# The down matrix by seven block products instead of plain tiles, with its block sums formed in the up stage

## The chip, the cores and the metric

The kernel runs on one core of one Trainium2 chip. The metric is the device time of one execution in microseconds (us). A run of the kernel before took 1713.6 us (median of 3 runs, 1712.56 to 1714.36).

## The reference, cut to what matters

The reference is a decoder block over 1024 tokens of width 1024: two kinds of attention, gates, an output projection, and then a two-matrix network with a squared ReLU. All is float32. What bears on this change is the last part:

```
h = _rms_norm(x, norm_mlp_g)                     # (1024 tokens, 1024)
x = x + square(relu(h @ w_up)) @ w_down          # w_up 1024 x 4096, w_down 4096 x 1024
return _rms_norm(x, norm_final_g)
```

Call U = square(relu(h @ w_up)) the hidden matrix, 4096 rows (transposed: hidden features are rows, tokens are columns) by 1024 tokens.

## The kernel before

Everything is kept transposed, features on the 128 partitions and tokens along the free axis. A float32 product is made from three matrix products of rounded parts: each operand X is split into X_hi (a rounded copy, made by ScalarE) and X_lo = X - X_hi (made by VectorE), and hi·hi + hi·lo + lo·hi is summed in PSUM. So "three matmuls of 128x512" is the unit of work: one 128x128 block of weights against 512 tokens.

**The up stage** (1021 to 1338 us in the trace) works in 16 blocks, n = 0 to 15, each of 256 hidden features. Each block is a 2x2 block product (2 halves of 128 features, 2 halves of the 1024 tokens, the inner 1024 cut in 2 halves of 512) done with Strassen's method in Winograd's form: seven block products P1 to P7 in place of eight. A product is 4 inner tiles x 3 parts = 12 matmuls (`product`, L1084). Their order over the blocks is in `up_products`: in block n it is P1(n), P7(n-1), P3(n-2), P6(n), P4(n-1), P2(n), P5(n). Inputs: the four weight blocks a11, a12, a21, a22 are loaded, VectorE forms four sums of them (`sums`, L1856), ScalarE makes the hi parts of three groups (`form_hi`, L1443) and VectorE the lo parts (`form_lo`, L1886). Outputs: running sums sit in PSUM. ScalarE copies P1 (`copy_s1`, L1451), P1+P6 (`copy_s2`, L1459) and P1+P6+P7 (`copy_s3`, L1467) out. VectorE adds them up, applies ReLU and the norm's factor (`up_c22`, `up_r22`, `up_c12`, `up_r12`, `up_r21`, `up_r11`), ScalarE squares (L1471), and SyncE's queue stores the four 128x512 results of each block to the DRAM buffer `hidden`. Every engine runs its list in the written order, and a wait holds back all that is behind it on its engine.

**The down stage** (1338 to 1686 us) is plain: 8 chunks of 512 hidden features, and in each 8 output tiles of 128 features: 4 inner tiles x 3 parts x 2 token halves = 24 matmuls per tile (L1118), 64 tiles, 1536 matmuls. Hidden tiles come back from DRAM (`load_hidden`), are split (`hidden_hi` L1491, `hidden_lo` L1856), the weights likewise (`weights_hi` L1487, `weights_lo` L1856). VectorE adds each tile into the residual in `keep` (L1856). In the last chunk ScalarE squares the finished tiles (L1570) and VectorE sums the squares into `f_acc`. Then a short tail forms the final norm: `facc` complete, 8 small matmuls, root and reciprocal, 64 transposes (L1130), eight scaled results and their stores.

Of the kernel before, what the change touches and what calls it, by code (L numbers as in the profile page):

```python
# [25 lines left out]
ALU = mybir.AluOpType  # L26
ACT = mybir.ActivationFunctionType
BF16 = mybir.dt.bfloat16
F32 = mybir.dt.float32
# [3 lines left out]
P = 128  # L33
# [30 lines left out]
DN_PAIRS = (3, 2, 1, 0)  # L64
DN_BANKS = (1, 3, 0, 2)
# [3 lines left out]
def up_products(n):  # L69

    if n == 0:
        order = [(0, P1), (0, P2), (0, P6), (0, P5)]
    elif n < UP:
        order = [(n, P1), (n - 1, P7), (n - 2, P3), (n, P6), (n - 1, P4), (n, P2), (n, P5)]
    else:
        order = [(n - 1, P7), (n - 2, P3), (n - 1, P4), (n - 1, P3)]
    return [x for x in order if x[0] >= 0]


PRODUCT = {x: i + 1 for i, x in enumerate(x for n in range(UP + 1) for x in up_products(n))}  # L80
A_FORMS = [(0, 0), (0, 1), (0, 2), (1, 0), (1, 1)]
for _n in range(1, UP):
    A_FORMS += [(q, b) for q, b in ((_n + 1, 0), (_n, 2), (_n + 1, 1)) if q < UP]
A_FORM = {x: i + 1 for i, x in enumerate(A_FORMS)}
H_FORMS = [(w, k) for k in range(3) for w in ("b11", "b21", "t2")]
H_FORMS += [("b11", 3), ("t13", 0), ("t13", 1), ("t13", 2), ("t4b", 0), ("b21", 3), ("t2", 3), ("t13", 3), ("t4b", 1),
            ("t4b", 2), ("t4b", 3)]
H_FORM = {x: i + 1 for i, x in enumerate(H_FORMS)}

# [92 lines left out]
def build(nc, x, g_attn, w_in, b_forget, w_branch, w_out, g_mlp, w_up, w_down, g_final, rope, f_rows, x_mid, hidden, out):  # L182
# [4 lines left out]
    w_dn_v = w_down.rearrange("(f p) n -> p f n", p=P)  # L187
# [3 lines left out]
    with ExitStack() as ctx:  # L191
# [23 lines left out]
        up_t4b = [at(f"up_t4b_{k}", [P, 2, 2, HALF], F32R, 32 + 8 * k) for k in range(4)]  # L215
# [6 lines left out]
        W_KB = (184, 192, 80, 88)  # L222
        dn_w = [at(f"dn_w{i}", [P, 2, 1024], F32R, W_KB[i]) for i in range(4)]
        dn_w_raw = [at(f"dn_w_raw{i}", [P, 1024], F32, W_KB[i] + 4) for i in range(4)]
        HID_KB = (64, 72, 96, 104, 0, 8, 16, 24)
        dn_h = [at(f"dn_h{i}", [P, 2, 1024], F32R, HID_KB[i]) for i in range(8)]
        dn_h_raw = [at(f"dn_h_raw{i}", [P, 1024], F32, HID_KB[i] + 4) for i in range(8)]
        f_sq = [at(f"f_sq{i}", [P, 1024], F32, 168 + 4 * i) for i in range(2)]
        f_acc = at("f_acc", [P, 1024], F32, 176)
        f_g = at("f_g", [P, 1024], F32, 180)  # L230
        y_tile = [at(f"y{i}", [P, 1024], F32, (144, 148, 152, 156, 160, 164, 200, 204)[i])[:] for i in range(8)]
# [93 lines left out]
        def bank_b(q):  # L325
            return ps_bank(6 + q % 2)
# [21 lines left out]
        rstd_l, rstd_r = kp[:, 0, left], kp[:, 0, right]  # L348
        s2 = [kp[:, 1, left], kp[:, 1, right]]
        s1 = [kp[:, 2, right], kp[:, 4, right]]  # L350
        s3, u12 = kp[:, 3, left], kp[:, 3, right]
        u11 = [kp[:, 2, left], kp[:, 2, right]]
        u22 = [kp[:, 4, left], kp[:, 4, right]]
        u21 = [kp[:, 5, left], kp[:, 5, right]]
# [87 lines left out]
        x_back = [sem(f"x_back{i}") for i in range(4)]  # L442
# [32 lines left out]
        u21_out = [sem(f"u21_out{i}") for i in range(2)]  # L475
        u12_out = sem("u12_out")
        dw_in = [sem(f"dw_in{i}") for i in range(4)]
        dw_hi = sem("dw_hi")
        dw_lo = sem("dw_lo")
        dh_hi = sem("dh_hi")  # L480
        dh_lo = sem("dh_lo")
        dn_done = sem("dn_done")
        dn_add = sem("dn_add")
# [14 lines left out]
        def _(sp):  # L498
# [50 lines left out]
            def load_a(q, what):  # L549
                e, m = {"a11": (0, 0), "a12": (1, 0), "a21": (0, 1), "a22": (1, 1)}[what]  # L550
                sp.dma_start(a_block(q, what).rearrange("p (k c) -> p k c", k=4),
                             w_up_v[:, 4 * e:4 * e + 4, (2 * q + m) * P:(2 * q + m + 1) * P]).then_inc(a_in[q % 4], 16)

            def load_hidden(f):

                q = f // 2
                if f % 2 == 0:
                    sp.wait_ge(u11_out[q % 2], 16 * (q // 2 + 1))
                    sp.wait_ge(u12_out, 16 * (q + 1))
                else:  # L560
                    sp.wait_ge(u21_out[q % 2], 16 * (q // 2 + 1))
                    sp.wait_ge(u22_out[q % 2], 16 * (q // 2 + 1))
                sp.dma_start(dn_h_raw[f % 8][:], hidden[f]).then_inc(tile_in[f % 8], 16)

            def load_dn(g):
                b, pair = g // 4, DN_PAIRS[g % 4]
                sp.dma_start(dn_w_raw[g % 4][:].rearrange("p (k c) -> p k c", k=4),
                             w_dn_v[:, 4 * b:4 * b + 4, pair * 256:(pair + 1) * 256]).then_inc(dw_in[g % 4], 16)

            def store_u22(q):  # L570
                sp.wait_ge(u22_ok, q + 1)
                sp.dma_start(hidden[2 * q + 1, :, right], u22[q % 2]).then_inc(u22_out[q % 2], 16)

            def store_u12(q):
                sp.wait_ge(u12_ok, q + 1)
                sp.dma_start(hidden[2 * q, :, right], u12).then_inc(u12_out, 16)

            def store_u21(q):
                sp.wait_ge(u21_ok, q + 1)
                sp.dma_start(hidden[2 * q + 1, :, left], u21[q % 2]).then_inc(u21_out[q % 2], 16)  # L580

            def store_u11(q):
                sp.wait_ge(u11_ok, q + 1)
                sp.dma_start(hidden[2 * q, :, left], u11[q % 2]).then_inc(u11_out[q % 2], 16)

            def reload(m):
                for i in range(2):
                    sp.wait_ge(x_out[i], (64, 48)[i])
                sp.dma_start(kp[:, m, :], x_mid[m]).then_inc(x_back[m // 2], 16)
# [10 lines left out]
            for n in range(KC):  # L600
# [12 lines left out]
                else:  # L613
                    if n >= 2:
                        sp.wait_ge(x_out[n % 2], 16 * (n // 2))
                    sp.wait_ge(resid, n + 1)
                    sp.dma_start(x_mid[OUT_ORDER[n]], kp[:, OUT_ORDER[n], :]).then_inc(x_out[n % 2], 16)

            for n in range(UP):
                q = n + 2  # L620
                if q < UP:
                    sp.wait_ge(done, PRODUCT[n, P1])
                    load_a(q, "a11")
                elif n == UP - 1:
# [1526 lines left out]
```

## Time and profile before

| what | value |
|---|---|
| median of 3 runs | 1713.6 us |
| the profiled execution's own time | 1710.07 us |
| its span, first to last instruction | 1708.3 us |
| TensorE (PE) busy | 1623.1 us, 95% |
| VectorE (DVE) busy | 970.9 us, 57% |
| ScalarE (ACT) busy | 749.7 us, 44% |
| mean granted TensorE clock | 0.987 |

The profile lists, for each engine, how long its instructions ran and, where it sat idle, which engine's instruction ended the wait. A matmul of 512 columns shows 389 ns of its own but the next one starts before it ends, so its price is the distance between starts.

### The profile page before, as it was taken

The page shows a single profiled execution, that of the slowest core. Times are in us where ns is not written, and L with a number is a line of the kernel's source. Part 1 is how long each engine was busy: PE and PEld are TensorE (multiplying, and loading weights), DVE is VectorE, ACT ScalarE, POOL GpSimd, SP SyncE. Part 2 cuts the span into 40 slices and gives each one's busy share as a digit, 9 for nine tenths or more (in the row PEclk, how much of TensorE's full clock was granted, in tenths as well). Part 3 has the DMA queues.
Part 4 walks back from the last instruction along what each step waited for, and adds up shares of the span by engine and source line. Part 5 has one row for each costly group of instructions (what it writes and reads, how often), then busy time and mean ns, then how long its engine had stood idle before and what let it go on. Part 6 is the DMA issues. An engine that isn't in the chain of part 4 may idle for free.

```text
span 1708.3 us, 22294 instructions
## 1 busy us (share of the span) xinstructions
PE 1623.1 (95%) x8024; PEld 1337.6 (78%) x8024; DVE 970.9 (57%) x1917; ACT 749.7 (44%) x1602; POOL 4.1 (0%) x20
## 2 busy tenths in 40 slices
PE   6998998997899999999999998999999999999997
PEld 5777776775688887788888887888888888888886
DVE  5688888875666666522215566555555544444445
ACT  6566777783667666511113454433344311111111
POOL 0000000000000000000000000000000000000000
PEclk9999999999899999999999999999999999999998
DMA  5210110010010200011121542333334622222212
GB/s 173 87 38 26 32 32 25 26 38 13 13 51 13 63 26 23 14 54 44 51 60 52 148 124 80 118 119 116 105 105 143 227 99 99 99 99 98 93 33 99
DMA packets 142487, 126.19 MB, mean 74 GB/s; under 512 B 5160, under 2 KB 124968, under 8 KB 142256
## 3 DMA queue, kind: packets, MB, share of 16 engines
q1 hardware_dynamic: 142384, 124.84, 23.0%
q8 instruction: 62, 1.02, 0.2%
q14 instruction: 41, 0.34, 0.1%
HBM read 100.15 MB, written 24.67 MB: 73 GB/s over the span
## 4 chain that ended last, share of the span: by engine, by line
PE 79%; DVE 10%; ACT 5%; issue 5%; DMA 0%; ACTq 0%; DVEq 0%; SPq 0%
PE ps L1118 20%; PE ps L1084 18%; PE ps L759 17%; PE ps L803 12%; PE ps L875 4%; PE ps L842 2%; DVE work L1669 2%; PE ps L853 2%; ACT work L1266 1%; DVE ps L1690 1%; DVE o_nat L1712 1%; ACT tmp L1258 1%; DVE tmp L1654 1%; PE ps L748 1%; DVE work L1697 1%
## 5 line engine op out<-in xcount | busy, mean ns | idle before, releaser
L803 PE MATMUL ps<-hspl,wsp 128*128 128x512 f32 x1536 | 423.1, 408 | 8.4 <-ACT tmp L1222 6.8
L1118 PE MATMUL ps<-dn_h,dn_w 128*128 128x512 f32 x1536 | 348.3, 389 | 0.0
L1118 PEld LDWEIGHTS ps<-dn_h,dn_w 128*128 128x128 f32 x1536 | 288.4, 188 | 59.8
L803 PEld LDWEIGHTS ps<-hspl,wsp 128*128 128x128 f32 x1536 | 266.2, 190 | 54.7 <-ACT tmp L1222 8.6
L759 PE MATMUL ps<-hspl,wsp 128*128 128x512 f32 x960 | 222.6, 392 | 0.6 <-ACT keep L1288 0.6
L759 PEld LDWEIGHTS ps<-hspl,wsp 128*128 128x128 f32 x960 | 181.1, 189 | 38.4 <-issue 0.8
L1856 DVE TENSOR_TENSOR keep<-keep,ps 128x1024 f32<-128x1024 f32 x72 | 87.8, 1220 | 161.0 <-PE ps L1118 146.9
L875 PEld LDWEIGHTS ps<-work 128*128 128x128 f32 x856 | 112.0, 191 | 47.7 <-issue 37.7
L1258 ACT ACTIVATE tmp<-ps,negmax 128x128 f32<-128x128 f32 (+7 forms) x160 | 87.5, 547 | 125.8 <-DVE negmax L1690 123.9
L1697 DVE TENSOR_TENSOR work<-ps,work 128x128 fp32r<-128x128 f32 (+3 forms) x192 | 84.4, 454 | 102.5 <-ACT work L1266 99.9
L875 PE MATMUL ps<-work 128*128 128x128 f32 x856 | 122.5, 276 | 21.2 <-DVE o_nat L1712 20.1
L1084 PE MATMUL ps<-up_b,a_hi 128*128 128x512 f32 x384 | 120.5, 395 | 4.9 <-DVE up_b L1856 3.8
L1241 ACT ACTIVATE work<-tmp 64x128 fp32r<-64x128 f32 x320 | 113.3, 354 | 5.9
L1669 DVE SCALAR_TENSOR_TENSOR work<-tmp,work 64x128 fp32r<-64x128 f32 x320 | 101.3, 317 | 9.2 <-ACT work L1241 1.8
L1491 ACT CAST dn_h<-dn_h_raw 128x1024 fp32r<-128x1024 f32 x32 | 33.3, 1048 | 146.6 <-DMA dn_h_raw<-hidden 146.5
L842 PE MATMUL ps<-work 128*128 128x256 f32 (+3 forms) x384 | 88.8, 326 | 3.1 <-issue 2.1
L1084 PEld LDWEIGHTS ps<-up_b,a_hi 128*128 128x128 f32 x384 | 73.3, 191 | 21.0 <-DVE up_b L1856 4.2
L1471 ACT ACTIVATE keep<-keep 128x512 f32<-128x512 f32 x64 | 40.4, 631 | 98.4 <-DVE keep L2013 41.1
L853 PE MATMUL ps<-ident,tmp 128*128 128x128 f32 x428 | 73.7, 274 | 10.2 <-issue 6.9
L1847 DVE TENSOR_TENSOR wsp<-raw,wsp 128x1024 fp32r<-128x1024 f32 x18 | 22.0, 1223 | 105.9 <-ACT wsp L1386 105.9
L1084 PE MATMUL ps<-up_t,a_hi 128*128 128x512 f32 x256 | 79.1, 390 | 0.0
L1084 PE MATMUL ps<-up_t4b,a_hi 128*128 128x512 f32 x256 | 78.8, 389 | 0.0
(201 smaller groups left out, 2138.7 us busy)
## 6 DMA issues: line engine op xcount, KB each, us to landing
raw<-in_w_in SPq DMA_DIRECT2D x47, 512.0 KB, 3.8
hidden<-keep SPq DMA_DIRECT2D x64, 256.0 KB, 2.3
dn_w_raw<-in_w_down SPq DMA_DIRECT2D x32, 512.0 KB, 3.5
dn_h_raw<-hidden SPq DMA_DIRECT2D x32, 512.0 KB, 6.4
a_raw<-in_w_up SPq DMA_DIRECT2D x36, 256.0 KB, 2.8
spare<-in_w_up SPq DMA_DIRECT2D x28, 256.0 KB, 3.2
keep<-in_x SPq DMA_DIRECT2D x8, 512.0 KB, 7.0
fbias<-f_rows SPq DMA_DIRECT2D x8, 512.0 KB, 4.9
```

Of the source, the lines that this page charges most:

```text
L759: ins = pe.matmul(ps[:, cols], w(wp, k), mv(mp, k)[:, cols], start=(k == 0 and n == 0), stop=(k == ks - 1 and n == 2))
L803: ins = pe.matmul(psp(u, g), wsp[c % 2][:, wp, k * P:(k + 1) * P], hspl[:, mp, k, cols], start=(n == 0), stop=(n == 23), skip_group_check= ...
L842: ins = pe.matmul(oo, lt, rh, start=(m == 0), stop=(m == len(ops) - 1), skip_group_check=True)
L853: ins = pe.transpose(PS[2][:, (u % 2) * HALF + (k - a) * P:(u % 2) * HALF + (k - a + 1) * P], probs(G)[:, k * P:(k + 1) * P], ident[:])
L875: ins = pe.matmul(o, pt[:, G % 2, part, n * P:(n + 1) * P], v_nat[:, j, s % 2, :, :].rearrange("p s d -> p (s d)"), start=(part == 0 and n ...
L1084: ins = pe.matmul(o, a_part(q, j, wp)[:, k * P:(k + 1) * P], b_block(j, mp, k), start=((j in (P1, P5) or j == P2 and q < 2) and k == 0 and ...
L1118: ins = pe.matmul(o[:, cols], dn_w[g % 4][:, wp, a:a + P], dn_h[(4 * b + f) % 8][:, mp, cols], start=(f == 0 and n == 0), stop=(f == 3 and ...
L1241: act.activation(tile_view(q_st[dst:dst + 64, G % 3, 0, :], t), tile_tokens(q_raw(t)[row:row + 64], t, s // 2), ACT.Copy, scale=-QSCALE).t ...
L1258: act.activation(probs(G)[:, 0:n * P], psc[G % 2][:, 0:n * P], ACT.Exp, bias=negmax[:, c:c + 1], scale=-1.0, accum_out=rowsum[:, c:c + 1]) ...
L1669: dve.scalar_tensor_tensor(out=tile_view(q_st[dst:dst + 64, G % 3, 1, :], t), in0=tile_tokens(q_raw(t)[row:row + 64], t, s // 2), scalar=- ...
L1697: dve.tensor_tensor(pt[:, G % 2, 1, a * P:b * P], PS[2][:, (u % 2) * HALF:(u % 2) * HALF + (b - a) * P], pt[:, G % 2, 0, a * P:b * P].bitc ...
L1856: return dve.tensor_tensor(out, a, b, op)
```

## The change

The down matrix gets the same treatment as the up matrix. There are 32 more blocks, n = 16 to 47: 8 chunks of 512 hidden features, and in each chunk 4 blocks of 2x128 output features. One product of a down block has 2 inner tiles x 3 parts = 6 matmuls. One function `product` now serves both stages, and `block_products` gives the order. P5 of all chunks stays in PSUM, where it is summed over the chunks (banks 2 to 5); the four other results (P1+P2 as "11", "22", "12", "21") are added by VectorE to the residual in every block.

The moving inputs of the down products are 7 forms of each chunk of the hidden matrix: four blocks of it (for P1, P2, P3 and, through them, the rest) and four block sums, T1 to T4. The sums are formed in the up stage by VectorE (`t_sums`, four new 128x512 operations in each block) and stored, so `hidden` now has seven 128x512 tiles per block where it had four. `u21` has one buffer instead of two, and the places of the temporaries in `keep` are dealt anew. In the down stage each of the 7 forms of a chunk is loaded (`load_form`, 512 KB), rounded by ScalarE (`dn_hi`, 128x1024) and its remainder formed by VectorE (`dn_lo`, 128x1024). The down weights go through the up stage's `sums`, `form_hi` and `form_lo`, one unit of 1 MB for two blocks. The split of the up matrix's form "t4b", first tile, moves behind `form_lo(1, 1)` on both engines.

```diff
-def up_products(n):
+def block_products(n):
     if n == 0:
+        return [(0, P1), (0, P2), (0, P6), (0, P5)]
+    if n <= UP:
         order = [(n, P1), (n - 1, P7), (n - 2, P3), (n, P6), (n - 1, P4), (n, P2), (n, P5)]
+        order += [(n - 1, P3)] if n == UP else []
+    elif n == UP + 1:
+        order = [(n, P1), (n - 1, P7), (n, P6), (n - 1, P4), (n, P2), (n, P5), (n - 1, P3)]
     else:
+        order = [(n, P1), (n - 1, P7), (n - 1, P3), (n, P6), (n - 1, P4), (n, P2), (n, P5)]
...
+    early = {UP - 1: [(0, P1)], UP: [(0, P6), (0, P2), (0, P5), (0, P7)], UP + 1: [(0, P4), (0, P3), (1, P1)],
+             UP + 2: [(1, P6)], UP + 3: [(1, P2), (1, P5), (1, P7)], UP + 4: [(1, P4), (1, P3)]}
...
+    c, pos = divmod(n - UP, 4)
+    c += 1 if pos else 0
+    if c < 2 or c > 7:
+        return []
+    return [(c, j) for j in ((P3,), (P1, P6, P2), (P5,), (P7, P4))[pos]]
...
         @block.tensor
...
+            def product(n, j):
...
+                down = n >= UP
+                pe.wait_ge(a_lo, A_FORM[form_of(n), form_place(j)[0]])
+                if down and (n - UP) % 4 == 0:
+                    pe.wait_ge(b_lo, D_FORM[(n - UP) // 4, j])
                 if j == P1:
...
+                        pe.wait_ge(c21_ok, n - 1)
...
+                elif j == P4:
+                    if down:
+                        pe.wait_ge(c22_ok, n + 1)
...
+                ks = 2 if down else 4
...
-            for i in range(8 * FF_BLOCKS):
...
         @block.scalar
...
+            copy_s1(UP)
+            dn_hi(0, P6)
             copy_s3(UP - 1)
             square_22(UP - 1)
             square_12(UP - 2)
+            dn_hi(0, P2)
+            copy_s2(UP)
+            dn_hi(0, P5)
+            form_hi(UP, 2)
             square_21(UP - 1)
+            dn_hi(0, P7)
+            copy_s1(UP + 1)
             square_12(UP - 1)
+            dn_hi(0, P4)
...
+            for n in range(UP + 2, NB):
+                forms = dn_forms(n)
+                copy_s1(n)
+                if n % 2:
+                    for x in forms[:2]:
+                        dn_hi(*x)
+                    if form_of(n) + 1 < N_FORM:
+                        form_hi(form_of(n) + 1, 0)
+                        form_hi(form_of(n) + 1, 1)
+                    for x in forms[2:]:
+                        dn_hi(*x)
+                    copy_s2(n)
+                    if form_of(n) + 1 < N_FORM:
+                        form_hi(form_of(n) + 1, 2)
+                else:
+                    for x in forms:
+                        dn_hi(*x)
+                    copy_s2(n)
+                for i in final_events(n):
+                    final_square(i)
...
         @block.vector
...
+            def t_sums(q, ops=(1, 2, 3, 4)):
...
+                        dve.wait_ge(u12_ok, q + 1)
...
+                        ins = add(t3, u22[q % 2], u12, ALU.subtract)
...
+                        ins = add(t2, t3, u11[q % 2])
...
+                        ins = add(u12, u12, u11[q % 2], ALU.subtract)
...
+                        ins = add(t4, u21, t2, ALU.subtract)
...
                 if n >= 2:
                     up_r12(n - 2)
+                    t_sums(n - 2)
                 up_r21(n - 1)
+                form_lo(n + 1, 1)
+                if n == UP - 1:
+                    dn_lo(0, P1)
                 up_r11(n)
+            sums(UP + 1)
+            dn_lo(0, P6)
             up_c22(UP - 1)
             up_r22(UP - 1)
             up_c12(UP - 2)
             up_r12(UP - 2)
+            dn_lo(0, P2)
+            dn_lo(0, P5)
+            t_sums(UP - 2)
             up_r21(UP - 1)
+            dn_add(UP, "11")
+            form_lo(UP, 2)
+            dn_lo(0, P7)
             up_c12(UP - 1)
             up_r12(UP - 1)
+            dn_lo(0, P4)
+            dn_add(UP, "22")
...
+            for n in range(UP + 2, NB + 1):
+                forms = dn_forms(n)
...
+                elif n % 2 == 0:
+                    form_lo(u - 1, 2)
+                    if more:
+                        sums(u, (1,))
+                    if n > UP + 2:
+                        dn_add(n - 1, "22")
+                    if more:
+                        sums(u, (2,))
+                    dn_add(n - 1, "12")
+                    if more:
+                        sums(u, (3, 4))
+                    dn_add(n - 1, "21")
+                    for x in forms:
+                        dn_lo(*x)
+                    dn_add(n, "11")
+                else:
+                    for x in forms[:2]:
+                        dn_lo(*x)
+                    dn_add(n - 1, "22")
+                    if more:
+                        form_lo(u, 0)
+                    dn_add(n - 1, "12")
+                    if more:
+                        form_lo(u, 1)
+                    dn_add(n - 1, "21")
+                    for x in forms[2:]:
+                        dn_lo(*x)
+                    dn_add(n, "11")
+                if NB > n > NB - 4:
+                    dn_last(n - 1, "22")
+                    dn_last(n - 1, "12")
+                for i in final_events(n):
+                    final_sum(i)
...
         @block.sync
...
+            def load_unit(u):
+                sp.wait_ge(a_lo, A_FORM[u - 2, 2])
+                load_a(u, "a21")
+                load_a(u, "a22")
+                sp.wait_ge(done, last_use(u - 2, P1))
+                load_a(u, "a11")
+                sp.wait_ge(done, last_use(u - 2, P2))
+                load_a(u, "a12")
...
+            for n in range(UP + 3, NB):
+                c, pos = divmod(n - UP, 4)
+                if pos % 2 and form_of(n) + 2 < N_FORM:
+                    load_unit(form_of(n) + 2)
+                if pos == 0 and c < 7:
+                    for j in D_ORDER:
+                        load_form(c + 1, j)
```

## Rows read from the trace of the kernel before

**Rows 1.** The page, busy time of each engine over the span, and instructions.
```profile
PE 1623.1 (95%) x8024; PEld 1337.6 (78%) x8024; DVE 970.9 (57%) x1917; ACT 749.7 (44%) x1602; POOL 4.1 (0%) x20
```
**Rows 2.** Busy time by stretch: up stage, down stage, tail (columns: length, engines, clock, DMA, GB/s).
```profile
1021.48:1337.90 316.42, 311.54 (x1377) 257.69 (x1376) 183.70 (x224) 129.81 (x174) 0.00 (x0) 0.99 0.35 115
1337.90:1686.20 348.30, 348.30 (x1537) 288.20 (x1535) 153.30 (x131) 64.91 (x65) 0.00 (x0) 1.00 0.27 96
1686.20:1708.30 22.10, 12.51 (x81) 12.05 (x80) 12.72 (x12) 1.26 (x2) 0.00 (x0) 0.77 0.47 191
```
**Rows 3.** Waits after 1330 us: who waited for whom (total us, times, longest).
```profile
DVE keep L1856 <- PE ps L1118: 146.9, 55, 4.2
```
**Rows 4.** TensorE's two waits in the up stage.
```profile
1030.20 1.22 PE L1084 MATMUL ps<-up_b,a_hi 128*128 128x512 f32 x2 [3.80 <-DVE up_b L1856]
...
1049.46 0.70 PE L1084 MATMUL ps<-up_b,a_hi 128*128 128x512 f32 x2 [1.08 <-ACT keep L1451]
```
**Rows 5.** Instructions of line 1118, the down matmuls.
```profile
L1118 PE MATMUL ps<-dn_h,dn_w x1536: 388/389/389, 1337.9 to 1685.8; 128*128 128x512 f32 x192
```
**Rows 6.** TensorE in order of time: first matmuls of P1(9) and of P7(8).
```profile
1193.74 0.62 PE L1084 MATMUL ps<-up_b,a_hi 128*128 128x512 f32 x2
...
1196.46 0.62 PE L1084 MATMUL ps<-up_t,a_hi 128*128 128x512 f32 x2
```
**Rows 7.** VectorE in order of time in that block (start, length, what, idle before).
```profile
1194.02 0.69 DVE L1856 TENSOR_TENSOR a_raw<-spare 128x512 f32<-128x512 f32 x1 [2.10 <-DMA a_raw<-in_w_up]
1194.74 0.69 DVE L1856 TENSOR_TENSOR spare<-a_raw,spare 128x512 f32<-128x512 f32 x1
1195.35 0.68 DVE L1856 TENSOR_TENSOR a_raw<-a_raw,a_raw 128x512 f32<-128x512 f32 x1
...
1200.67 1.22 DVE L1886 TENSOR_TENSOR a_lo<-a_raw,a_hi 128x1024 fp32r<-128x1024 f32 x1
1201.80 0.69 DVE L2013 SCALAR_TENSOR_TENSOR keep<-keep 128x512 f32<-128x512 f32 x1
...
1204.56 1.76 DVE L1886 TENSOR_TENSOR a_lo<-spare,a_hi 128x1536 fp32r<-128x1536 f32 x1 [1.47 <-ACT a_hi L1443]
...
1207.55 0.69 DVE L2020 SCALAR_TENSOR_TENSOR keep<-ps,keep 128x512 f32<-128x512 f32 x1 [0.63 <-PE ps L1084]
```
**Rows 8.** ScalarE in order of time in that block.
```profile
1196.66 0.57 ACT L1451 COPY ps<-ps 128x512 f32<-128x512 f32 x1 [4.08 <-PE ps L1084]
1197.15 1.05 ACT L1443 CAST a_hi<-a_raw 128x1024 fp32r<-128x1024 f32 x1
...
1203.06 1.47 ACT L1443 CAST a_hi<-spare 128x1536 fp32r<-128x1536 f32 x1
...
1206.95 0.63 ACT L1471 ACTIVATE keep<-keep 128x512 f32<-128x512 f32 x1 [1.54 <-DVE keep L2031]
```
**Rows 9.** The page, DMA issues: kilobytes each, median us from issue to landing.
```profile
hidden<-keep SPq DMA_DIRECT2D x64, 256.0 KB, 2.3
...
dn_h_raw<-hidden SPq DMA_DIRECT2D x32, 512.0 KB, 6.4
a_raw<-in_w_up SPq DMA_DIRECT2D x36, 256.0 KB, 2.8
```
**Rows 10.** VectorE at the head of the up stage.
```profile
1021.24 1.22 DVE L1856 TENSOR_TENSOR up_t4b<-keep,up_t4b 128x1024 fp32r<-128x1024 f32 x1
```
**Rows 11.** Busy time and clock by stretch: an attention stretch, after the long wait, around the short.
```profile
200.00:300.00 100.00, 88.44 (x474) 69.34 (x473) 83.44 (x255) 72.53 (x212) 0.00 (x0) 1.00 0.10 27
...
1030.00:1032.00 2.00, 1.80 (x4) 1.49 (x5) 1.79 (x4) 1.22 (x2) 0.00 (x0) 0.50 0.00 0
...
1048.00:1050.00 2.00, 0.92 (x4) 0.48 (x3) 1.97 (x4) 1.78 (x3) 0.00 (x0) 1.00 0.16 54
```
**Rows 12.** TensorE in order of time at the end: the first small matmul of the mean.
```profile
1689.89 2.31 PE L1124 MATMUL ps<-mean_w,f_acc 128*128 128x1 f32 x16 [3.66 <-DVE f_acc L1856]
```
**Rows 13.** The chain that ended last, in order of time: matmuls after the 3.80 us wait.
```profile
1030.20 6.37 PE ps L1084 x15
```

More of the change, by code:

```diff
@@ L346, in a_block, with dn_tiles, dn_out @@
             return third_raw(q)[:, {"a21": 0, "s3": 0, "a22": 1, "s4": 2}[what], :]
[L348 to L354, printed above, removed]
+        s1 = [kp[:, 0, left], kp[:, 0, right]]
+        u11 = [kp[:, 1, left], kp[:, 4, right]]
+        u22 = [kp[:, 1, right], kp[:, 6, left]]
+        s2 = [kp[:, 2, left], kp[:, 4, left]]
+        s3 = kp[:, 2, right]
+        rstd_l, rstd_r = kp[:, 3, left], kp[:, 3, right]
+        u12, t2 = kp[:, 5, left], kp[:, 5, right]
+        t3 = kp[:, 6, right]
+        u21, t4 = kp[:, 7, left], kp[:, 7, right]
+        def dn_tiles(n):
+            pos = (n - UP) % 4
+            first = pos // 2 * 4 + pos % 2
+            return first, first + 2
+        def dn_out(n, what):
+            return kp[:, dn_tiles(n)[int(what[0]) - 1], (left, right)[int(what[1]) - 1]]
         def to_natural(g, copy, eng):
@@ L474, in build @@
         u22_out = [sem(f"u22_out{i}") for i in range(2)]
[L475 to L483, printed above, removed]
+        u21_out = sem("u21_out")
+        t_ok = sem("t_ok")
+        t1_out = sem("t1_out")
+        t2_out = sem("t2_out")
+        t3_out = sem("t3_out")
+        t4_out = sem("t4_out")
+        b_hi = sem("b_hi")
+        b_lo = sem("b_lo")
+        fin12 = sem("fin12")
+        fin22 = sem("fin22")
         fsq = sem("fsq")
@@ L1081, in product @@
+                first = j == P1 or j == P5 and n < UP + 4 or j == P2 and n < 2
+                o = bank_b(n) if j == P2 else bank_c(n) if j == P5 else bank_e(n) if j == P3 else bank_a(n)
+                ks = 2 if down else 4
+                for k in range(ks):
+                    if n == 0:
                         pe.wait_ge(hf_lo, H_FORM[{P1: "b11", P2: "b21", P6: "t2", P5: "t13", P7: "t13", P4: "t4b",
@@ L1525, in _ @@
             form_hi(1, 1)
-            for k in range(1, 4):
+            for k in range(4):
                 h_hi("t4b", k)
             act.wait_ge(rstd_done, 1)
-            act.copy(kp[:, 0, :], PS[2][:]).then_inc(rstd_out, 1)
+            act.copy(kp[:, 3, :], PS[2][:]).then_inc(rstd_out, 1)
             square_11(0)
@@ L1982, in _ @@
             dve.reciprocal(xrstd[:], xstat[:]).then_inc(rstd_ok, 1)
-            for k in range(1, 4):
+            for k in range(4):
                 h_lo("t4b", k)
@@ new lines, in dn_last, with final_sum @@
+            def dn_last(n, what):
+                dve.wait_ge(done, PRODUCT[n, P5])
+                if what == "12":
+                    dve.wait_ge(c12_ok, n + 1)
+                else:
+                    dve.wait_ge(c22_ok, n + 1)
+                o = dn_out(n, what)
+                add(o, o, bank_c(n)).then_inc(fin12 if what == "12" else fin22, 1)
+            def final_sum(i):
+                half = int(FINAL[i][1][1]) - 1
+                cols = (left, right)[half]
+                dve.wait_ge(fsq, i + 1)
+                if i == 0:
+                    dve.wait_ge(gfin_in, 16)
+                    link(dve.memset(f_acc[:], 0.0))
+                else:
+                    dve.wait_ge(facc, i)
+                add(f_acc[:, cols], f_acc[:, cols], f_sq[:, i % 4, :]).then_inc(facc, 1)
```

547 lines of the change are left out of this document (273 added, 274 removed).

## The prediction

> **What bounds the kernel now.** I read the busy times first: TensorE (PE) works 95% of the span, VectorE 57%, ScalarE 44% [rows 1]. The question is whether that holds in the two stages touched, so next comes the table by stretch: PE is busy 311.5 of 316.4 us in the up stage and for all of the 348.3 us of the down stage, at full clock [rows 2]. Then the waits: in the down stage VectorE waits for PE 55 times, at most 4.2 us [rows 3], and nothing makes PE wait before the end. So down there only fewer or cheaper matmuls count, and PE has cover: VectorE is at 153 of 348 us, ScalarE at 65. The two waits of PE in the up stage are at its head [rows 4].
>
> **Removed.** 64 tiles x 24 = 1536 matmuls took 348.3 us, 0.2268 us each [rows 2, 5]. The new stage has 32 blocks x 7 products x 6 = 1344. The 192 fewer are worth 192 x 0.2268 = 43.5 us. The up stage shows that this price holds when products alternate: P1(9) to P7(8) is 2.72 us for 12 matmuls [rows 6]. A product in the down stage is half of that, 1.36 us, a block 9.53 us.
>
> **What must fit into 9.53 us.** VectorE, for two down blocks (19.05 us): 8 additions, 4 weight sums at 0.69 us, three weight remainders (1.22, 1.22, 1.76), and 3.5 hidden remainders at 1.22 [rows 7]: 5.5 + 2.8 + 4.2 + 4.3 = 16.8 us, 88%. ScalarE: four copies at 0.57, roundings 1.05 + 1.05 + 1.47, and 3.5 at 1.05 [rows 8]: 9.5 us, 50%. Both fit on average; the order decides. Two handovers come from rows: PE's product is seen by ScalarE 0.20 us after the next one starts (1196.46 to 1196.66) [rows 6, 8], by VectorE the same, and a VectorE operation of 512 columns lets the next start after 0.61 us, one of 1024 after 1.13 [rows 7]; on ScalarE a copy of 0.57 gives way after 0.49 [rows 8], and I take 0.95 for a rounding of 1.05.
>
> **An even block** (time 0 is the start of its P1; its slots are P1 to 1.36, P7 of the block before to 2.72, P3 to 4.08, P6 to 5.44, P4 to 6.80, P2 to 8.17, P5 to 9.53). VectorE: third weight remainder, first weight sum, then "22", for which P7 is done at 2.91. The sum waits for the weight block a12, asked for when P2 is done, at -1.2; with 2.8 us to landing [rows 9] it runs at 1.7 to 2.4, "22" at 2.9 to 3.6, and P4, which needs it, starts at 5.44. Slack 1.8 us. "21" ends at 7.7, needed by the next P1 at 9.53. No cost.
>
> **An odd block.** ScalarE first copies P1 (1.55 to 2.12), then rounds two hidden forms (2.04 to 3.09, 2.99 to 4.04). VectorE makes their remainders (3.11 to 4.33, 4.25 to 5.47), and only then "22" (5.39 to 6.08). P4 waits for it: it starts at 6.15 instead of 5.44, 0.7 us late. This is the queue at work: "22" could run at 2.9 but stands behind two remainders, which stand behind ScalarE. After it the weight remainders end at 8.9 and "21" at 9.6, while the next P1 is now due at 10.25. Blocks with two or more early forms: 19, 21, ... 43, that is 13. Cost 13 x 0.72 = 9.4 us. Bounds: 0, if the handovers are shorter than I take them, and 13 x 1.5 = 20 us with every link 0.2 us slower.
>
> **The seam**, blocks 15 to 19, where little can be done ahead because the old stage holds the buffers. I write out the lists of the diff with the durations above; time 0 is the start of P1(16), and old products still last 2.72 us.
> - P1(16) needs the first hidden remainder. "21" of 14 ends 1.8 us before block 15 does, its square takes 0.6, the rounding 1.05, the remainder 1.2: 1.1 us late, with the form's load landing just in time 1.3.
> - P2(16), due at 10.9: VectorE has the sums of unit 17 until 5.1 (a12 lands late, at 2.4), a remainder, "22" of 15, then "12" of 14 until 9.1; its square ends at 9.8, the rounding of form P2 at 10.7, the remainder at 11.95: 1.1 late.
> - P7(16), due at 18.9: four `t_sums` 13.3 to 16.0, "21" of 15, one addition to 17.2, the 1.76 us form to 18.9, the remainder to 20.05: 1.2 late.
> - P4(16), due at 22.8: "12" of 15 to 21.3, its square to 21.95, rounding to 22.9, remainder to 24.1, "22" to 24.75: 2.0 late.
> - P7(17) and P6(18), each behind a ScalarE copy: 0.25 each.
> - P1(19), due at 40.1: "22" of 17 to 34.1, two `t_sums`, a remainder, a form to 38.1, four weight sums and "12" to 41.4, "21" to 42.05: 2.0 late.
>
> Sum 8.1; I take 8.0. Bounds: 0 (no wait of VectorE or ScalarE reaches PE), and 16: a link late by 1 us passes through each of some eight waits, and the reloads of the residual share the DMA with the first forms.
>
> **The up stage.** Added per block on VectorE: four sums of 0.69, 2.8 us, on 10.7 of 19.05 (183.7 of 316.4 us in the stage [rows 2]). They stand ahead of "21", which goes from 1207.55 to about 1211 on the scale of rows 7: the first of them waits for the square of "12", ending at 1207.58 [rows 8], and four follow at 0.61 to 0.72. P1(10) is due at 1193.74 + 19.05 = 1212.8, so 1.1 to 1.8 us of slack are left: no cost. The queue moves too: the load of a12 stands behind the four stores and goes about 1.8 us later, the sums then run at 1195.8, and what follows them waits until 1200 for a ScalarE copy anyway. The stores grow by three of 256 KB per block; each lands in 2.3 us [rows 9], and a buffer is wanted again 19 us later (`u21`, now single: stored at about +18.2, wanted at +35.5). If this cover were gone, it would be up to 15 x 1 us; the lower bound is 0.
>
> **The head.** The first "t4b" remainder leaves its place ahead of the residual addition: 1.14 us [rows 10] less on the path to the 3.80 us wait [rows 4]. The clock was 0.50 after that wait [rows 11]; whether 2.7 us of idleness leave it up, no row says. I take -1.1, bounds -2.5 and 0. The 1.08 us wait stays: its chain starts at PE's spreading of the factor.
>
> **The end.** The last three products P7, P3, P4 of block 47 have a chain: "22", its last part, "12", its last part, "21", then three half-size sums of squares. VectorE comes out of block 47's squares 3.5 us late and holds P4(47) by 1.5 us; from P4's end to the mean it is 3.4 us, before 3.66 [rows 12]; block 46 adds 0.3. Together +1.6, bounds 0 and 4.
>
> **Sum** on the profiled execution: 1708.3 - 43.5 + 9.4 + 8.0 - 1.1 + 1.6 = 1682.7 us of span. Around the span lie 1710.07 - 1708.3 = 1.8, and the median of the runs shown is 3.5 above that execution's own time: 1688.0.
>
> **A rule that speaks against the change.** In an attention stretch PE is busy 88% of 100 us and the granted clock is 1.00; it was 1.00 around the 1.08 us wait, and 0.50 after the 3.80 us one [rows 4, 11]. The Trainium skill, "TensorE: Matmul & The Clock Gate", section "A second HAM failure mode: psum-queue depth-cycling", says that frequent tiny idle gaps between groups of matmuls, with PSUM banks cycled, can make the clock swing between its two levels and cost throughput. By that rule the new down stage, with a gap in every second block, would swing, and the time would be that of rival 4; the attention stretch, idle 12% of the time, speaks against it.
>
> **Rivals.**
> 1. *No new waits*: ScalarE and VectorE keep ahead, the orders cost nothing. 1708.3 - 43.5 - 1.1 + 5.3 = 1669. For it: 12% and 50% of free time. Against it: the chain copy, two roundings, two remainders is longer than 5.44 us by sums of rows. 12%.
> 2. *Weights late*: a12 lands like the hidden loads, 6.4 us after its issue [rows 9], as the forms of the next chunk are asked for right behind it. The first sum then ends at 5.9, "22" at 6.6, P4 is 1.2 us late in each of some 13 even blocks too: +16, 1704. Against it: 2.8 us where other transfers run beside it. 18%.
> 3. *VectorE is the bound*: 16.8 us of work in 19 with gaps forced by waits for PE; if each pair of blocks takes 20.8 instead of 19.8, 16 more: 1704. 8%.
> 4. *The clock falls* (the side of slower): place, the waits of 0.7 to 2 us in the down stage and seam; price, after the long wait 15 matmuls took 6.4 us instead of 15 x 0.227 = 3.4 [rows 13], so 3 us a time. The gain left is 25.6 us: from nine falls in the 20 waits on, the kernel is slower; with all, 1688 + 60 = 1748. Against it: the clock of 1.00 beside waits [rows 11]. 5%.
>
> **Numbers.** Forecast 1688 us (57%; its own range 1679 to 1697), rivals as given. The range, 8 in 10, takes in the bounds on both sides: 1673 to 1705. A measurement tells 0.2%, 3.4 us, from no change: faster 0.93, within 0.02, slower 0.05.
>
> **What would show it.** Right: 1344 matmuls of the down stage at 0.227 us; PE waits of about 0.7 us ahead of P4 in every odd block up to 43, ended by VectorE's addition; seven waits in the seam, 8 us in all; no wait of PE in blocks 2 to 14; the head's wait at 2.7 us. Wrong: waits of ScalarE or VectorE for a12 that reach PE in even blocks (rival 2), waits ahead of P1 (rival 3), clock under 1.0 in the down stage (rival 4), or PE at work without a gap (rival 1).

## The result, and the profile after

The changed kernel takes 1704.34 us (median of 4, 1703.57 to 1705.92) against 1713.98 (median of 4, 1712.56 to 1715.10) before: a ratio of 0.9949, 95% interval 0.9937 to 0.9962. It is faster, as forecast, but by 9.6 us instead of 25.6. The profiled execution has an own time of 1703.57 us and a span of 1701.7.

Busy times on the page of the changed kernel, and its DMA issues (KB each, median us from issue to landing):
```profile
PE 1593.1 (94%) x7832; PEld 1304.0 (77%) x7832; DVE 1114.0 (65%) x2165; ACT 831.9 (49%) x1714; POOL 4.1 (0%) x20
...
dn_raw<-hidden SPq DMA_DIRECT2D x56, 512.0 KB, 5.6
```
192 matmuls are gone [rows 1], as the arithmetic says. The table by stretch (start and end, length, PE, PEld, DVE, ACT, POOL, clock, DMA share, GB/s) puts the three stretches of [rows 2] beside it. The second here begins at P1(16), the first product of the down matrix; four products of the up stage still lie behind it.
```profile
1026.36:1332.38 306.02, 299.78 (x1330) 247.65 (x1328) 212.85 (x276) 124.97 (x164) 0.00 (x0) 0.99 0.44 147
1332.38:1679.33 346.95, 323.79 (x1392) 260.80 (x1392) 267.03 (x326) 151.77 (x185) 0.00 (x0) 0.99 0.43 147
1679.33:1701.70 22.37, 12.95 (x82) 12.01 (x80) 13.35 (x15) 1.44 (x3) 0.00 (x0) 0.82 0.47 188
```
What the reader is to see: before, PE had no idle time in its down stage [rows 2]. Now 23.2 of 347 us of the second stretch are idle, and VectorE's share of it is 77%, where it was 44%.

**A correction before any comparison.** The first product of the up stage starts at 1026.36 us; before, it was 1021.48. PE's work ahead of that point is the same, so these 4.9 us are not of the change. They are clock: in the same stage, which is not touched, the granted clock of six microseconds is 1.00 in the one execution and 0.54 in the other, and PE issues 44 matmuls in it or 25. Over 380 to 472 us PE starts 412 matmuls in the one and 382 in the other, and behind that, 500 to 1020 us, no fewer (2666 and 2676). First the kernel before, then the changed one:
```profile
466.00:472.00 6.00, 6.00 (x44) 5.36 (x42) 3.49 (x10) 3.88 (x12) 0.00 (x0) 1.00 0.01 3
```
```profile
466.00:472.00 6.00, 6.00 (x25) 5.01 (x24) 2.48 (x8) 1.95 (x6) 0.00 (x0) 0.54 0.00 0
```
Over all profiles of this study that point lies between 1021.5 and 1027.7 us. So I count from it on: 1708.3 - 1021.48 = 686.8 us before, 1701.7 - 1026.36 = 675.3 us after. In this pair of profiles the change gives **11.5 us**, the forecast said 25.6, and 14.1 us are to be found. A second profile of the changed kernel (e0 below) has 678.8 us from that point on, 3.5 more, so differences of this size between two profiles show nothing by themselves.

PE's waits in order of time (start, length of the group, engine and line, in brackets the idle time before it and its releaser). The first line is the head's wait, the next eight are the seam:
```profile
1034.17 0.76 PE L1170 MATMUL ps<-up_b,a_hi 128*128 128x512 f32 x2 [2.89 <-DVE up_b L1944]
...
1332.38 0.70 PE L1170 MATMUL ps<-dn_b,a_hi 128*128 128x512 f32 x2 [2.27 <-issue]
...
1345.00 0.71 PE L1170 MATMUL ps<-dn_b,a_hi 128*128 128x512 f32 x2 [1.16 <-issue]
...
1347.92 0.70 PE L1170 MATMUL ps<-dn_b,a_hi 128*128 128x512 f32 x2 [1.30 <-issue]
...
1354.77 0.70 PE L1170 MATMUL ps<-dn_b,a_hi 128*128 128x512 f32 x2 [1.17 <-issue]
...
1359.60 0.70 PE L1170 MATMUL ps<-dn_b,a_hi 128*128 128x512 f32 x2 [1.83 <-DVE keep L1944]
...
1377.20 0.70 PE L1170 MATMUL ps<-dn_b,a_hi 128*128 128x512 f32 x2 [1.83 <-DVE keep L1944]
...
1379.76 0.70 PE L1170 MATMUL ps<-dn_b,a_hi 128*128 128x512 f32 x2 [0.95 <-ACT ps L1526]
...
1388.83 1.19 PE L1170 MATMUL ps<-dn_b,a_hi 128*128 128x512 f32 x2 [4.71 <-DVE keep L1944]
...
1410.79 0.70 PE L1170 MATMUL ps<-dn_b,a_hi 128*128 128x512 f32 x2 [0.63 <-DVE keep L1944]
...
1430.74 0.70 PE L1170 MATMUL ps<-dn_b,a_hi 128*128 128x512 f32 x2 [0.63 <-DVE keep L1944]
```
Behind the head's, they stand ahead of P1(16), P2(16), P5(16), P7(16), P4(16), P1(19), P7(18), P4(18), then P4(20) and P4(22). And PE's waits between 1395 and 1640 us, summed (total us, times, longest):
```profile
PE ps L1170 <- DVE keep L1944: 7.5, 12, 0.6
```
Twelve waits of 0.63 us, one in every second block, ended by VectorE's addition. That is the picture forecast for the odd blocks. The 4.71 us wait was not in the forecast; it is the first of the thirteen odd blocks, 19, and it is also followed by a slower clock: 1.19 us for the first two matmuls instead of 0.70.

### The profile page after: what moved, and what is told of

The parts are those of the page before. It is cut to its first block, busy times and chain, and to the rows that moved or that the text cites. A ratio compares the mean times of both kernels' runs of the same rounds, so it can differ in the third digit from the quotient of the medians.

```text
span 1701.7 us, 22848 instructions
## 1 busy us (share of the span) xinstructions
PE 1593.1 (94%) x7832; PEld 1304.0 (77%) x7832; DVE 1114.0 (65%) x2165; ACT 831.9 (49%) x1714; POOL 4.1 (0%) x20
## 4 chain that ended last, share of the span: by engine, by line
PE 71%; DVE 14%; issue 6%; ACT 6%; DMA 2%; SPq 0%; ACTq 0%; DVEq 0%
PE ps L1170 30%; PE ps L833 17%; PE ps L877 12%; PE ps L949 4%; PE ps L916 2%; DVE work L1757 2%; PE ps L927 2%; DVE keep L1944 1%; DVE dn_b L1944 1%; ACT work L1326 1%; DVE ps L1778 1%; DVE o_nat L1800 1%; ACT dn_b L1554 1%; ACT tmp L1318 1%; DVE tmp L1742 1%
## 5 line engine op out<-in xcount | busy, mean ns | idle before, releaser
L1170 PE MATMUL ps<-dn_b,a_hi 128*128 128x512 f32 x896 | 279.7, 393 | 25.4 <-DVE keep L1944 18.4
L1170 PEld LDWEIGHTS ps<-dn_b,a_hi 128*128 128x128 f32 x896 | 167.3, 189 | 68.9 <-issue 34.0
L1170 PE MATMUL ps<-dn_b,a_lo 128*128 128x512 f32 x448 | 175.2, 391 | 0.0
L1944 DVE TENSOR_TENSOR keep<-keep,ps 128x512 f32<-128x512 f32 (+1 forms) x144 | 101.3, 712 | 35.6 <-PE ps L1170 20.9
L1944 DVE TENSOR_TENSOR dn_b<-dn_raw,dn_b 128x1024 fp32r<-128x1024 f32 x56 | 67.3, 1221 | 50.8 <-ACT dn_b L1554 50.7
L1170 PEld LDWEIGHTS ps<-dn_b,a_lo 128*128 128x128 f32 x448 | 84.5, 189 | 17.9
L1980 DVE TENSOR_TENSOR a_lo<-a_raw,a_hi 128x1024 fp32r<-128x1024 f32 (+1 forms) x66 | 81.3, 1234 | 11.0 <-ACT a_hi L1504 10.9
```

What stands on the lines that cost most here:

```text
L1170: ins = pe.matmul(o, a_part(n, j, wp, k), b_block(n, j, mp, k), start=(first and k == 0 and m == 0), stop=(k == ks - 1 and m == 2), skip_g ...
L1944: return dve.tensor_tensor(out, a, b, op)
L1980: dve.tensor_tensor(a_lo_t[q % 2][b][:], src[:], a_hi_t[q % 2][b][:].bitcast(F32), ALU.subtract).then_inc(a_lo, 1)
```

## The experiments

Each was timed in 5 rounds with the kernel before on the same chip. My theory after the result: the gain went into waits of PE that come from the *order* of VectorE's, ScalarE's and SyncE's lists, not from the amount of work. Its rivals: VectorE has too much to do (its busy time rose by 143 us), or the clock. "From P1(0)" is the profiled span less the start of P1(0), one profile for each; the changed kernel's first profile had 675.3.

| run | median us | ratio to before, 95% | from P1(0) us |
|---|---|---|---|
| before | 1713.0 to 1713.5 | 1 | 686.8 |
| e0_changed_again | 1703.91 | 0.9939 [0.9925, 0.9954] | 678.8 |
| e1_22_first | 1690.78 | 0.9871 [0.9857, 0.9886] | 665.1 |
| e2_forms_early | 1696.16 | 0.9897 [0.9883, 0.9911] | 668.4 |
| e3_hi_first | 1698.57 | 0.9913 [0.9900, 0.9926] | 669.5 |
| e4_three | 1681.86 | 0.9807 [0.9791, 0.9823] | 655.5 |
| e5_p1_form_early | 1702.62 | 0.9944 [0.9931, 0.9957] | 676.1 |
| e6_tsums_1col | 1701.18 | 0.9932 [0.9918, 0.9946] | 672.0 |
| e7_all_five | 1681.57 | 0.9813 [0.9794, 0.9831] | 652.6 |
| e8_p6_form_early | 1677.70 | 0.9795 [0.9780, 0.9810] | 651.1 |
| e9_end_22_first | 1679.36 | 0.9804 [0.9790, 0.9818] | 651.6 |

**e0_changed_again**: the changed kernel once more, for the spread.

> The changed kernel itself, as the yardstick on this chip: about 1704 us, ratio to the kernel before about 0.995. From block 0 to the end of the up stage and on, PE's waits as in its first trace: 12 of 0.63 us in odd down blocks, 4.7 us ahead of P4(18).

Its six runs lie between 1696.80 and 1705.84. The wait ahead of P4(18) was 6.27 us in its profile where it had been 4.71: the size of that wait is not fixed, its place is. From P1(0) on this profile takes 678.8 us, the first one 675.3.

**e1_22_first**: in the odd blocks, the addition that P4 waits for goes ahead of the two remainders.

```diff
+                    dn_add(n - 1, "22")
                     for x in forms[:2]:
                         dn_lo(*x)
-                    dn_add(n - 1, "22")
```

> One thing undone: in odd down blocks VectorE's addition of "22" no longer stands behind two hidden remainders. My theory (the wait is the queue behind ScalarE's two roundings): the 12 waits of 0.63 us, 0.79 from start to start, go, the wait ahead of P4(18) shrinks to nearly nothing too, since "22" of 18 no longer stands behind late forms, but P2/P5-type products of block 20 may then wait for the late forms instead. Steady part alone: 12 x 0.79 = 9.5 us less than the changed kernel, 1695; with the wait ahead of P4(18) and its slow clock up to 16 less, 1688. Rival (VectorE is full, the wait only moves to P1 of the next block): 1702 to 1704.

The ratio falls by 0.0068, some 12 us. The stretch 1400 to 1640 us of the changed kernel, then of this one:
```profile
1400.00:1640.00 240.00, 232.47 (x1013) 188.87 (x1012) 188.16 (x226) 107.16 (x127) 0.00 (x0) 1.00 0.41 141
```
```profile
1400.00:1640.00 240.00, 240.00 (x1058) 197.22 (x1057) 195.07 (x235) 112.33 (x133) 0.00 (x0) 1.00 0.41 136
```
PE has no gap left, with VectorE busy 195 of 240 us (81%) instead of 188. So VectorE's load is not what cost time there: order is, and the rival "VectorE is the bound" falls for this stretch. In block 19 the same edit takes the 4.71 us wait away, but 2.08 us now stand ahead of P7(18) and 2.33 ahead of P1(20): there the late thing is something else (e2).

**e2_forms_early**: five of the second chunk's hidden loads in SyncE's list go ahead of the weight loads of unit 18, and all seven ahead of the last stores and four reloads.

```diff
-            load_form(1, P1)
+            for j in (P1, P6, P2, P5, P7):
+                load_form(1, j)
             load_unit(UP + 2)
+            load_form(1, P4)
+            load_form(1, P3)
...
-            load_form(1, P6)
...
-            for j in (P2, P5, P7, P4, P3):
-                load_form(1, j)
```

> One thing moved: SyncE's queue asks for the seven forms of chunk 1 ahead of the four reloads and the last up stores, some 20 us earlier. My theory (the forms of chunk 1 are late only because they stand behind reloads in the queue): the wait of 4.71 us ahead of P4(18) falls to the 0.6 us of other odd blocks, the clock stays up after it (2.1 us), the 0.95 us ahead of P7(18) goes: 7 us less than the changed kernel, 1697. Rival (the DMA engines are full around the seam, order is nothing): the loads then delay the weights of unit 18 or the reloads, and the time stays within 1 us, 1704.

SyncE's list in the changed kernel (start, length, what): the load asked for first there and the group of five, behind the last stores and reloads.
```profile
1371.69 0.95 SPq L639 DMA_DIRECT2D hidden<-keep  x1
1372.76 0.82 SPq L624 DMA_DIRECT2D dn_raw<-hidden  x1
1374.44 2.46 SPq L652 DMA_DIRECT2D keep<-x_mid  x3
1377.02 3.12 SPq L624 DMA_DIRECT2D dn_raw<-hidden  x5
```
ScalarE there, waiting for these loads to land, and VectorE, waiting for ScalarE:
```profile
1378.08 1.05 ACT L1554 CAST dn_b<-dn_raw 128x1024 fp32r<-128x1024 f32 x1 [8.54 <-DMA dn_raw<-hidden]
...
1384.45 1.04 ACT L1554 CAST dn_b<-dn_raw 128x1024 fp32r<-128x1024 f32 x1 [2.81 <-DMA dn_raw<-hidden]
```
```profile
1385.53 2.55 DVE L1944 TENSOR_TENSOR dn_b<-dn_raw,dn_b 128x1024 fp32r<-128x1024 f32 x2 [4.54 <-ACT dn_b L1554]
1388.00 0.68 DVE L1944 TENSOR_TENSOR keep<-keep,ps 128x512 f32<-128x512 f32 x1
```
The addition at 1388.00 is "22" of block 18, and P4(18) starts at 1388.83. Read backwards: P4(18), "22", two remainders, their roundings, a load that took 8.25 us to land, one of a pile of five. Ahead of that load SyncE's list had to wait for a store to land before it could go on to the last reload. Both in the chain of waits (start, length, what):
```profile
1371.69 4.83 DMA hidden<-keep
...
1377.51 8.25 DMA dn_raw<-hidden
```
In e2 that load is issued some 20 us earlier, in a group of five that starts at 1357.18 us. P4(18) there waits 0.64 us, at full clock, and the wait ahead of P7(18) is gone:
```profile
1384.23 0.70 PE L1170 MATMUL ps<-dn_b,a_hi 128*128 128x512 f32 x2 [0.64 <-DVE keep L1944]
```
The ratio falls by 0.0042, 7 us. What e1 cures at the end of this chain (the addition no longer behind the remainders), e2 cures at its start.

**e3_hi_first**: in the seam, the loads and roundings of chunk 0's forms go one place ahead of stores, copies and squares.

```diff
+            load_form(0, P5)
+            load_form(0, P7)
             store_u22(UP - 1)
-            load_form(0, P5)
-            load_form(0, P7)
...
+            dn_hi(0, P2)
             square_22(UP - 1)
             square_12(UP - 2)
-            dn_hi(0, P2)
-            copy_s2(UP)
             dn_hi(0, P5)
+            copy_s2(UP)
             form_hi(UP, 2)
-            square_21(UP - 1)
             dn_hi(0, P7)
+            square_21(UP - 1)
             copy_s1(UP + 1)
-            square_12(UP - 1)
             dn_hi(0, P4)
+            square_12(UP - 1)
```
(and `load_form(0, P4)` ahead of `store_t(UP - 2)`.)

> Orders at the seam: ScalarE rounds the forms P2, P7 and P4 of chunk 0 ahead of the squares they stood behind, and the loads of P5, P7 and P4 of chunk 0 stand ahead of the stores. My theory (VectorE idles three times 1.6 us there behind ScalarE): the waits ahead of P2(16), P5(16), P7(16), P4(16), 1.3 + 1.5 + 1.3 + 2.0 us, shrink by 3.5 to 5 us in all: 1700. Rival (VectorE's amount of work at the seam is what counts, idling or not): under 1 us, 1703 to 1704.

The waits ahead of P2(16) and P5(16) are gone, those of P7(16) and P4(16) are down from 1.17 and 1.83 to 0.49 and 0.37:
```profile
1332.85 1.19 PE L1170 MATMUL ps<-dn_b,a_hi 128*128 128x512 f32 x2 [2.26 <-issue]
...
1352.77 0.70 PE L1170 MATMUL ps<-dn_b,a_hi 128*128 128x512 f32 x2 [0.49 <-issue]
...
1356.12 0.71 PE L1170 MATMUL ps<-dn_b,a_hi 128*128 128x512 f32 x2 [0.37 <-DVE keep L1944]
```
The ratio falls by 0.0026 only, 4.5 us: the clock fell after the first wait here (1.19 us for two matmuls; from P1(16) to P7(16) PE needs about 1.5 us more than its matmuls and the 0.49 us wait account for), and 2.30 us stand ahead of P7(18), where it had been 0.95.

**e4_three**: the three edits together.

> The three orders of the first experiments together ("22" first in odd blocks, forms of chunk 1 early, roundings at the seam ahead of the squares). If the three costs are separate: the changed kernel's 1704 less 10.3 (13 waits of 0.79), less 7 (late forms and the slow clock after them), less 5: 1681 to 1682. If they share a cause (VectorE at the seam is simply full), less is left than the sum: 1686 to 1690.

The ratio is 0.0132 below that of e0; the three alone make 0.0068 + 0.0042 + 0.0026 = 0.0136. By the timed runs they add up, as far as intervals of about 0.0014 on either side of each ratio can tell; by the profiles, counted from P1(0), the three alone save 22.9 us and together 19.8 against the first profile of the changed kernel, 33.4 and 23.3 against the second, so how far they add up stays open. P7(16) waits 1.13 us again here, 2.44 us stand ahead of P1(16), 0.88 ahead of P6(16), 1.84 ahead of P1(19) and 1.30 ahead of P1(20). Three orders, none of which removes an instruction, are worth more than the whole change was: 22.6 us.

**e5_p1_form_early**: on the changed kernel alone, in block 15 the first form's load goes ahead of all four weight loads, its rounding and its remainder one place up (the lines at their old places, which go, are not shown).

```diff
                 sp.wait_ge(done, PRODUCT[n, P1])
+                if n == UP - 1:
+                    load_form(0, P1)
...
+                if n == UP - 1:
+                    dn_hi(0, P1)
                 square_21(n - 1)
...
+                if n == UP - 1:
+                    dn_lo(0, P1)
                 form_lo(n + 1, 1)
```

> On the changed kernel, one thing: the form P1 of chunk 0 is asked for right after P1(15), ScalarE rounds it ahead of the square of "21" and VectorE takes its remainder ahead of the lo part of unit 16's second group. Theory (the 2.3 to 2.7 us ahead of P1(16) are that form's queue places alone): that wait goes, 2.4 us less, 1701.5. Rival (VectorE's backlog passes the wait on to P6(16) or P2(16)): within 0.5 us, 1704.

```profile
1335.88 0.70 PE L1170 MATMUL ps<-dn_b,a_hi 128*128 128x512 f32 x2 [2.39 <-issue]
```
The rival won: P1(16) does not wait any more, but P6(16), next in line with a form of its own, now waits 2.39 us, where it had started 0.2 us late. The time does not change clear of noise.

**e6_tsums_1col**: the four new sums per block on VectorE are cut to one column of 512. The kernel leaves the rest of T1 to T4 out, so its result is another one.

```diff
-                        ins = add(t2, t3, u11[q % 2])
+                        ins = add(t2[:, 0:1], t3[:, 0:1], u11[q % 2][:, 0:1])
```
(the other three likewise.)

> The changed kernel with VectorE's 64 new sums cut to one of 512 columns each (the sums T1 to T4 are left out but for that column, so the result is another); waits and stores stay. Theory (the new sums cost nothing in blocks 2 to 15, where VectorE has time, and something at the seam, where it has none): the pitch of an up block stays 19.04 us, PE's waits at the seam lose 2 to 4 us, 1701. Rival (the sums cost in the up stage): more than 5 us less, all before P1(16).

From P1(0) to where P1(16) is due it takes 303.3 us, and 303.6 us with the sums whole, though VectorE is busy 29 us less: they are hidden there, and "no cost" was right. In the seam the wait ahead of P4(16) goes from 1.83 to 1.37, that of P1(19) from 1.83 to 0.73, and that of P7(16) goes, while P1(16) waits 2.94 instead of 2.27. The profile gives 3.3 us, within the 3.5 by which two profiles of the changed kernel differ, and the timed runs cannot tell it from the changed kernel.

**e7_all_five**: e4 with e5, and "12", "21" of block 17 ahead of the sums in block 18.

> The three orders, the early P1 form, and in block 18 VectorE's "12" and "21" ahead of the four weight sums. If each wait is a matter of order: 1681.5 less 2.4 (ahead of P1(16)) less 2.0 (ahead of P1(19)): 1677. What then remains over 1344 x 0.2268 us is the end and one or two waits of under 1 us. If VectorE's work at the seam is the floor: 1681, the waits only changed places.

The median stays that of e4. The profile is 2.9 us shorter, which alone shows nothing, but its waits do: no wait ahead of P1(19), but 2.48 ahead of P6(16). The new order at block 18 does what was said; P1's wait only moves to P6, as in e5.

**e8_p6_form_early**: e7, with P6's load, rounding and remainder moved up in the same way.

```diff
                 load_a(q, "a22")
+                if n == UP - 1:
+                    load_form(0, P6)
...
+                if n == UP - 1:
+                    dn_hi(0, P6)
                 square_11(n)
...
+            dn_lo(0, P6)
             sums(UP + 1)
-            dn_lo(0, P6)
```

> The five orders and, as P1 before, the form P6 of chunk 0 asked for ahead of the stores of block 13's sums, rounded ahead of the square of "11", its remainder ahead of unit 17's sums. In the five-order kernel the P1 form's wait had only moved to P6(16), 2.6 us. Theory (two neighbouring forms, both needed, each behind the same stores): that wait goes, 2.6 us less from P1(0) on, 650; median 1679. Rival (VectorE's work is the floor, the wait moves on again to P2(16) or P5(16)): 652.6 us from P1(0) on, as before.

This kernel has the lowest median of the study: 1677.70 us (1675.31 to 1680.24), 0.9795 of the kernel before; its interval overlaps those of e4, e7 and e9. P6's wait is gone, and a new one of 1.01 us stands ahead of P2(16), again the next in line. By stretch:
```profile
1025.32:1328.65 303.33, 299.58 (x1329) 247.79 (x1328) 211.91 (x274) 124.74 (x164) 0.00 (x0) 0.99 0.44 146
1328.65:1654.11 325.46, 319.06 (x1393) 259.36 (x1391) 266.52 (x327) 151.71 (x185) 0.00 (x0) 1.00 0.46 158
1654.11:1676.40 22.29, 12.94 (x82) 12.02 (x80) 13.44 (x15) 1.44 (x3) 0.00 (x0) 0.82 0.47 189
```
PE is idle 6.4 us of the second stretch, where it was 23.2, with VectorE as busy as before.

**e9_end_22_first**: e8, with "22" of the last blocks ahead of the sums of squares of the block before (`adds_22` takes the place of the addition alone).

```diff
+            def adds_22(n, sums_of):
+                dn_add(n, "22")
+                for i in sums_of:
+                    final_sum(i)
```

> The same, and at the end VectorE adds "22" of blocks 45 to 47 ahead of the sums of squares of the block before. PE's waits ahead of P4(46) and P4(47), 0.9 and 1.9 us from start to start, go. Theory (at the end VectorE's own list to the last sum of squares is the path, PE's wait is only its shadow): PE ends its products 2.8 us earlier and waits 2 to 2.5 us longer for the mean; the time falls by 0.3 to 0.8 us. Rival (the waits of PE count): 2.8 us less.

The mean's first small matmul in e8, then in e9 (length, what, idle before it):
```profile
1657.63 2.94 PE L1184 MATMUL ps<-mean_w,f_acc 128*128 128x1 f32 x16 [3.27 <-DVE f_acc L1945]
```
```profile
1658.33 3.57 PE L1184 MATMUL ps<-mean_w,f_acc 128*128 128x1 f32 x16 [5.83 <-DVE f_acc L1945]
```
Both waits at the end, ahead of P4(45) and P4(47), are gone (the expectation names the first of them P4(46)), and the wait for the mean is longer by 2.6 us. The time is that of e8. The end is bound by VectorE's list: a wait of PE ahead of P4(47) costs nothing, since the sums put off are owed afterwards.

## Why the prediction came out as it did

The sign and the picture were right: PE busy, VectorE's and ScalarE's order as the new cost, none in blocks 2 to 14, 0.7 us in each odd block. (The 10.7 us of VectorE's work per up block that it read from [rows 2] are 11.1 by those rows; the slack is not used up by either.) The gain was 11.5 us on the same footing (8.0 with e0's profile), not 25.6. Point by point, times from start to start of the products:

| step | forecast us | measured us |
|---|---|---|
| 192 matmuls fewer | -43.5 | -43.5 |
| head | -1.1 | -2.0 |
| up stage, blocks 2 to 14 | 0 | 0 |
| odd blocks | 13 x 0.72 = 9.4 | 12 x 0.88 = 10.6 |
| seam | 8.0 | 19.1 |
| end | +1.6 | about +3.1 |

These make -12.7, against -11.5 measured. In the rows of the seam and the end a wait is counted as idle time plus 0.16 us, since the last matmul before it ends that much later than when the next follows at once. The first two matmuls behind it take 0.09 us longer as well, which for ten such waits makes 0.9 of the 1.2 us that are missing.

**The step that failed is the seam**, "Sum 8.1; I take 8.0". Its parts, forecast and measured: P1(16) 1.3 and 2.4; P6(16) none and 0.2; P2(16) 1.1 and 1.3; P5(16) none and 1.5; P7(16) 1.2 and 1.3; P4(16) 2.0 and 2.0; P7(17) and P6(18), 0.25 each, and 0.33 for P7(17) alone; P1(19) 2.0 and 2.0; P7(18) none and 1.1; P4(18), which I had at 0.72 as one of the thirteen odd blocks, 4.9 and 2.1 more for the slow clock behind it. Five entries are within 0.2 us of the lists written out by hand. In sum 19.1 us also lies above the seam's own upper bound of 16. What failed is what I did not write out: I followed VectorE's and ScalarE's lists and took the hidden loads as landed, while SyncE's list puts the second chunk's loads behind stores and three reloads. "The reloads of the residual share the DMA with the first forms" stood among the bounds and had no term. e2 shows it: the moved loads take 4.71 us down to 0.64. P5(16) and P7(18) were missed likewise: ahead of both ScalarE waits for a hidden load to land, 1.38 and 8.54 us. P1(16)'s load, taken to land just in time, kept ScalarE waiting for 0.93 us.

The **odd blocks** were right in mechanism and nearly in size, and e1 shows it by taking away the order and nothing else. The forecast had P4 start 0.72 us late. The idle time shown is 0.63, P4 starts 0.79 late, and two blocks take 19.93 us from wait to wait where 84 matmuls take 19.05: 0.88 for each.

The **head**: the wait went from 3.80 [rows 4] to 2.89 us, forecast 2.7, and the clock fell after it again (0.59 over 1034 to 1038 us), for a shorter time: the 15 matmuls behind it took 5.31 us by the chain of waits, before 6.37 [rows 13].

The **end** is about 1.5 us worse than forecast: waits of 0.72 and 1.77 us ahead of P4(45) and P4(47), with 3.26 us for the mean against 3.66 [rows 12].

**The rivals.** "No new waits" did not come about as the kernel stands, but e8 goes most of the way by order alone: 651.1 us from P1(0), 35.7 fewer than before, where the rival's sum has 44.6. "Weights late" did not happen in the steady part: no even block from 20 to 44 waits. In the seam a12 of unit 17 took 5.54 us to land and VectorE waited 2.62 us for it; the forecast had it landing 2.4 us after the start of P1(16), it landed at 3.1. "VectorE is the bound" falls by e1 in the odd blocks; in the seam e6 shows that less work shortens some waits, and e4 and e8 that order takes most of them away with the work left whole. "The clock falls" happened once in the down stage, after the 4.71 us wait. In the steady part it did not: 12 gaps in 240 us, clock 1.00 throughout (the table by stretch above). By that, the rule of the Trainium skill, "TensorE: Matmul & The Clock Gate", section "A second HAM failure mode: psum-queue depth-cycling", by which frequent small gaps between groups of matmuls make the clock swing, and which the prediction set beside this rival, is not borne out in this stretch: gaps of this size and number left the clock up.

## What to carry to other kernels

Where a change takes matmuls away and adds work to other engines, the gain can be decided, as here, less by how much these engines must do than by what stands ahead of what in each list; write out the lists of all of them, the DMA queue's too, for every stretch in which two stages overlap. An addition that frees a PSUM bank goes ahead of the preparation of operands that are wanted later (e1); at the end of the kernel, where the other engine's list was the path, the same move gave nothing (e9). A wait that is removed in front of one product may only move to the next with the same kind of input, so treat the whole run of products, and count from a point behind the code that did not change, with more than one profile of the same kernel.

## What the runs showed of the hardware that was not expected

- Code that did not change took 1021.5 to 1027.7 us, over the profiles of this study, with stretches at half clock that are in some executions and not in others (0.54 and 1.00 at 466 to 472 us above). That is over half of what this change gave.
- A wait of 2.26 us (e3) was followed by matmuls at half speed, 1.19 us for two, while waits of 2.27 us (the changed kernel, same place), 2.39 us (e5), 2.70 us (e1) and 2.94 us (e6) were followed by 0.70 us for two, full speed. The granted clock was 1.00 for 12 us behind each of these four. The length of the gap alone does not decide: a wait of 3.54 us (e3, ahead of P4(18)) left the clock at 1.00 too. Nor do the first two matmuls tell: behind waits of 3.84 us (e5) and 2.33 us (e1) they took 0.70 us, and the clock was at 0.50 some 2 us later.
- A hidden form of 512 KB lands in 5.6 us in the median, and one of a pile of five took 8.25 us.
